# Layout of the normed x, order of the router products, and engine of the second tile's split in a one-core decoder step

## The reference, cut to what matters

```python
x = layernorm(x, ln_in_g, ln_in_b)
proj = x @ w_in                          # all q, k, v, gates of both head groups
h = concat(mlstm(proj...), hgrn2(proj...))     # two recurrent mixers, states returned
x = layernorm(ALPHA * x + h @ w_out, ln1_g, ln1_b)
logits = x @ w_router + b_router         # 32 experts, the best 4 taken, softmax over them
ffn = sum over chosen experts of gate * (((up + 1) * glu) @ w_down + b_down)
ple = sigmoid(x @ w_ple_gate) * (p @ w_ple_proj)
x = layernorm(ALPHA * x + ffn + ple, ln2_g, ln2_b)
```

## Time and profile before

| | |
|---|---|
| median of 3 runs | 1274.18 us (1273.34 to 1274.27) |
| the profiled execution | 1272.39 us |
| its span | 1270.6 us |
| PE busy | 1170.6 us (92%) |
| DVE, ACT, POOL busy | 356.0, 201.1, 84.8 us |
| moved by DMA | 442.84 MB, mean 349 GB/s |
| granted TensorE clock, mean | 0.973 |

### The profile page before, as it was taken

How to read it: one execution, slowest core, us unless ns; L and a number is a source line. 1 busy time by engine, 2 the same in 40 slices (tenths; PEclk the granted TensorE clock), 3 DMA queues, 4 the chain that set the end, 5 groups by cost and what they waited for, 6 DMA issues and landing times.

```text
span 1270.6 us, 13173 instructions
## 1 busy us (share of the span) xinstructions
PE 1170.6 (92%) x5601; PEld 488.8 (38%) x5601; DVE 356.0 (28%) x566; ACT 201.1 (16%) x322; POOL 84.8 (7%) x91
## 2 busy tenths in 40 slices
PE   4999999599999997899999999999999999998984
PEld 3677874544232322233323232323233232322221
DVE  6865324441212121111212121212122221203114
ACT  1344234641010101011000010101010000110000
POOL 4200130211000021000000000000000000000000
PEclk9999999699999998999999999999999999999997
DMA  9751121569999999999999999999999999999992
GB/s 299 232 154 67 67 90 44 198 269 359 423 420 422 421 421 387 407 421 422 419 415 419 421 420 421 406 421 421 422 420 420 421 421 411 421 420 421 373 421 84
DMA packets 71357, 442.84 MB, mean 349 GB/s; under 512 B 8320, under 2 KB 8992, under 8 KB 22144
## 3 DMA queue, kind: packets, MB, share of 16 engines
q1 hardware_dynamic: 65984, 425.92, 82.4%
q0 software_dynamic: 5312, 16.04, 3.8%
HBM read 437.19 MB, written 4.73 MB: 348 GB/s over the span
## 4 chain that ended last, share of the span: by engine, by line
PE 68%; DMA 18%; DVE 7%; ACT 4%; issue 1%; SPq 1%; POOL 1%; DVEq 0%
PE ps L1021 40%; DMA ring<-in_w_up 12%; PE ps L605 9%; PE ps L1002 5%; DMA ring<-in_w_gate 4%; PE ps L954 3%; DVE y_s L1857 2%; DMA ring<-in_w_down 2%; ACT xb L1169 2%; PE ps L633 2%; DVE h_s L1855 1%; PE ps L1009 1%; ACT hTe L1169 1%; PE ps L823 1%; PE ps L1037 1%
## 5 line engine op out<-in xcount | busy, mean ns | idle before, releaser
L1021 PE MATMUL ps<-ring,xTe 128*64 128x512 f32 x1536 | 358.6, 601 | 19.5 <-DMA ring<-in_w_up 14.1
L1021 PEld LDWEIGHTS ps<-ring,xTe 128*64 128x64 f32 x1536 | 105.5, 136 | 244.4 <-issue 244.2
L1021 PE MATMUL ps<-ring,hTe 128*64 128x512 f32 x768 | 178.9, 604 | 7.7 <-DMA ring<-in_w_down 7.7
L1837 DVE TENSOR_TENSOR xs<-xs,ps 128x512 f32<-128x512 f32 x64 | 43.9, 687 | 346.8 <-PE ps L1002 346.8
L1021 PE MATMUL ps<-more,xTe 128*64 128x512 f32 x496 | 113.5, 598 | 2.7 <-DMA more<-in_w_gate 2.1
L605 PE MATMUL ps<-xT,ring 128*128 128x288 f32 x448 | 115.0, 413 | 1.0 <-PE ps L605 0.6
L1021 PEld LDWEIGHTS ps<-ring,hTe 128*64 128x64 f32 x768 | 51.7, 138 | 121.2 <-issue 120.8
L605 PEld LDWEIGHTS ps<-xT,ring 128*128 128x128 f32 x448 | 84.7, 193 | 25.1 <-issue 2.3
L1002 PE MATMUL ps<-y_s,GT 128*128 128x512 f32 (+1 forms) x256 | 82.0, 519 | 2.2 <-ACT y_s L1169 1.2
L1855 DVE TENSOR_SCALAR h_s<-ps 128x512 f32<-128x512 f32 x32 | 21.8, 681 | 160.9 <-PE ps L1021 160.9
L1169 ACT ACTIVATE h_s<-g_s 128x1024 f32<-128x1024 f32 x16 | 16.9, 1056 | 310.9 <-DVE g_s L1845 310.9
(11 more groups left out here) (366 smaller groups left out, 856.5 us busy)
## 6 DMA issues: line engine op xcount, KB each, us to landing
ring<-in_w_gate SPq DMA_DIRECT2D x96, 1024.0 KB, 11.3
ring<-in_w_up SPq DMA_DIRECT2D x96, 1024.0 KB, 11.7
ring<-in_w_down SPq DMA_DIRECT2D x96, 1024.0 KB, 13.6
more<-in_w_gate SPq DMA_DIRECT2D x32, 1024.0 KB, 9.8
more<-in_w_down SPq DMA_DIRECT2D x32, 1024.0 KB, 13.0
more<-in_w_up SPq DMA_DIRECT2D x30, 1024.0 KB, 13.1
ring<-in_w_in SPq DMA_DIRECT2D x28, 512.0 KB, 6.0
ring<-in_w_out SPq DMA_DIRECT2D x8, 512.0 KB, 5.0
```

The lines of the kernel that those rows point to most:

```text
L1021: last = mm(ps[64 * q:64 * q + 64, bank0 + half, :], lhs(k, q), wide(t)[:, k % 2, half * 512:(half + 1) * 512], start=False, stop=k == KT - 1)
L1837: tt(x, x, ps[:, CB_BANKS[n], 0:512 if i < 2 else QW], ALU.add).then_inc(S["cb_added"], 1)
```

## The change

1. `x1` of tiles 0 and 1 is written in step order (k p) by the norm's last instruction, which reads x and the bias with a stride of 8 elements. ACT's parts, the subtractions and PE's transposes of it are then contiguous; the router weights for tiles 0 and 1 are loaded by (p kt). Tile 2 stays in natural order and gets a second copy of the router weights, `w_rq`, in the old layout. `copy_sample_rows` reads PSUM with a stride and writes runs of 64. The experts' residual start (`xs <- ALPHA * x1`) reads x1 with a stride.
2. PE's order: transposes of tile 0 half way through project_out(1), route(0) behind it, then transpose_keys_b and project_out(2). A third bank set for the keys.
3. Tile 1's subtractions move from POOL to DVE. ACT copies `xT` of tile 0 between its parts, and writes tile 1's later parts behind the square root of tile 2. DVE selects tile 0 before the residual of tile 2.
4. `ln_q` is copied from the full gains by eight ACT copies per norm; its 24 DMAs are gone. POOL's first wait is for the gains (`ln1_in`) and no longer for the sample rows.
5. `transpose_v` uses three banks for the first set.
6. The number of extra blocks is read before pair 1; DVE spreads tile 2's statistics before the branch, and PE sums them before it.

```diff
-                for q in range(4):
-                    sp.dma_start(ln_q[q * NS:(q + 1) * NS, n, :],
-                                 a[v][q * QW:(q + 1) * QW].partition_broadcast(NS)).then_inc(S["ln1_in"], 16)
...
-            pool.wait_ge(S["x_in2"], 64)
+            pool.wait_ge(S["ln1_in"], 32)
...
-                load_quarters("ln1_g", "ln1_b")
...
+            pool.wait_ge(S["sA_ok"], 1)
+                pool.dma_start(w_rq[:, :, :], a["w_router"][0].rearrange("(kt p) n -> p kt n", p=P)).then_inc(S["router_in"], 16)
...
-            for i in range(2):
-                for q in range(2):
-                    rest(i, q)
+            for q in range(2):
+                pool.wait_ge(S["part_ok"], q + 1)
+                out = rests[:, 0, :]
+                nc.gpsimd.tensor_tensor(out, out if q else x1[:, 0, :], xb[:, 0, q, :], ALU.subtract).then_inc(S["rest_ok"], 1)
...
-            load_quarters("ln2_g", "ln2_b")
...
-                    if base + i >= 2:
-                        pe.wait_ge(S["v_ok"], base + i - 1)
+                    if banks[i] in banks[0:i]:
+                        pe.wait_ge(S["v_ok"], base + banks.index(banks[i]) + 1)
...
             project_out(0)
             transpose_keys_a()
-            project_out(1)
+            project_out(1, lambda: transpose_normed(0))
+            route(0)
             transpose_keys_b()
-            transpose_normed(0)
             project_out(2)
+            pe.wait_ge(S["kbt_ok"], 3)
             transpose_normed(1)
             row_stats(2)
-            route(0)
             transpose_normed(2)
...
+                if p == 1:
+                    pe.wait_ge(S["pos_ok"], 1)
+                    extra = pe.value_load(n_exti[0:1, 0:1], min_val=0, max_val=NXP)
...
-            extra = pe.value_load(n_exti[0:1, 0:1], min_val=0, max_val=NXP)
+            row_stats(3)
...
+            def copy_quarters(g, b):
+                for n, v in enumerate((g, b)):
+                    for q in range(4):
+                        rows_q = slice(q * NS, (q + 1) * NS)
+                        last = f(ln_q[rows_q, n, :], v[rows_q, q * QW:(q + 1) * QW], ACT.Copy)
+                last.then_inc(S["ln_q_ok"], 1)
...
-                    f(by_row(xb[:, i, q, :]), natural(rests[:, i, :] if q else x1[:, i, :]), ACT.Copy).then_inc(S["part_ok"], 1)
+                    f(xb[:, i, q, :], rests[:, i, :] if q else x1[:, i, :], ACT.Copy).then_inc(S["part_ok"], 1)
...
-            for q in range(3):
-                part(0, q)
+            part(0, 0)
+            part(0, 1)
+            copy_xT(0, 6, 0)
+            part(0, 2)
...
-            copy_xT(0, 6, 0)
             norm_scale(1, 5)
             part(1, 0)
             copy_xT(1, 6, 0)
             norm_scale(2, 6)
+            part(1, 1)
             part(2, 0)
             copy_xT(2, 6, 0)
-            part(1, 1)
             part(2, 1)
+            part(1, 2)
             part(2, 2)
-            part(1, 2)
...
+                if 4 <= n < 6:
+                    last = stt(x1[:, i, :].rearrange("r (k p) -> r k p", k=KT), by_step(x), mv[:, i, 3:4], by_step(b),
+                               ALU.mult, ALU.add)
...
-            mixer_residual(2)
-            norm(2, 6)
...
             select(0)
-            rest_of_samples(0)
+            mixer_residual(2)
+            tile_stats(2)
+            spread_stats()
+            rest_of(1, 0)
+            norm_stats(2, 6)
+            norm_apply(2, 6)
+            rest_of(1, 1)
+            rest_of(2, 0)
             select(1)
-            rest_of_samples(1)
+            rest_of(2, 1)
             select(2)
...
+                if i < 2:
+                    step(ts(xs[:, i, :].rearrange("r (p k) -> r p k", k=KT), by_row(x1[:, i, :]), ALPHA, None, ALU.mult))
...
-            extra = dve.value_load(n_exti[0:1, 0:1], min_val=0, max_val=NXP)
+            spread_stats()
```

More of the change, by code:

```diff
@@ L215, in trunk_step @@
         ident_b, ident_s = sb("ident_b", [P, P], BF16), sb("ident_s", [3 * NS, NS], BF16)
+        w_rq = over("w_rq", [P, KT, NE], "masks", 0, "masks")
         ext = over("ext", [P, NEXTRA, NE], "rows", 4 * 4 * NT, "rows")
@@ L287, in by_row, with by_step @@
             return t.rearrange("r (k p) -> r p k", k=KT)
-        def natural(t):
-            return t.rearrange("r (p k) -> r p k", k=KT)
+        def by_step(t):
+            return t.rearrange("r (p k) -> r k p", k=KT)
         def tokens(i):
@@ L489, in _ @@
             pool.wait_ge(S["numB_mm"], 1)
+            pool.wait_ge(S["sA_ok"], 1)
+            with nc.allow_non_contiguous_dma(reason="router weights by rows of 128 bytes"):
+                pool.dma_start(w_rq[:, :, :], a["w_router"][0].rearrange("(kt p) n -> p kt n", p=P)).then_inc(S["router_in"], 16)
             nc.gpsimd.tensor_tensor(S0[:, :, :, :], S0[:, :, :, :],
@@ L1192, in _, with copy_values @@
                 norm_scale(i, i + 1)
+            act.wait_ge(S["ln1_in"], 32)
+            copy_quarters(ln_g, ln_b)
             for i in range(3):
                 copy_xT(i, 0, 6)
-            def copy_values(base, bank0, off, width):
+            def copy_values(base, banks, off, width):
                 for i, (_, r) in enumerate(TILES):
@@ L1225, in _ @@
                       scale=DKA ** -0.5 if buf is QK and j >= 2 else 1.0).then_inc(S["proj_ok"], 1)
+                if c == 3:
+                    act.wait_ge(S["ln2_in"], 32)
+                    act.wait_ge(S["x_norm"], 3)
+                    copy_quarters(ln_g, ln_b)
                 if c == 4:
@@ L1374, in _ @@
             for p in range(NPAIR):
+                if p == 1:
+                    act.wait_ge(S["pos_ok"], 1)
+                    extra = act.value_load(n_exti[0:1, 0:1], min_val=0, max_val=NXP)
                 if p >= 1:
@@ L1400, in _ @@
             copy_y(NPAIR - 1)
-            extra = act.value_load(n_exti[0:1, 0:1], min_val=0, max_val=NXP)
             with act.If(extra > 0):
@@ L1774, in _, with rest_of @@
             norm(1, 5)
-            mixer_residual(2)
-            norm(2, 6)
+            def rest_of(i, q):
+                if i == 1:
+                    dve.wait_ge(S["part_ok"], 3 + q + 1)
+                    tt(rests[:, 1, :], rests[:, 1, :] if q else x1[:, 1, :], xb[:, 1, q, :], ALU.subtract).then_inc(S["later_rest_ok"], 1)
+                else:
+                    dve.wait_ge(S["partq_ok"], q + 1)
+                    tt(rest_q[:, :], rest_q[:, :] if q else x1q[:, :], xbq[:, q, :], ALU.subtract).then_inc(S["later_rest_ok"], 1)
             def select(i):
@@ L1921, in _ @@
             for i, (_, r) in enumerate(TILES):
-                step(ts(tokens(i), normed(i), ALPHA, None, ALU.mult))
+                if i < 2:
+                    step(ts(xs[:, i, :].rearrange("r (p k) -> r p k", k=KT), by_row(x1[:, i, :]), ALPHA, None, ALU.mult))
+                else:
+                    step(ts(xq[:, :], x1q[:, :], ALPHA, None, ALU.mult))
             for p in range(NPAIR):
+                if p == 1:
+                    dve.wait_ge(S["pos_ok"], 1)
+                    extra = dve.value_load(n_exti[0:1, 0:1], min_val=0, max_val=NXP)
                 if p == 0:
```

71 lines of the change are left out of this document (32 added, 39 removed).

## The result

Median 1253.67 us (1252.57 to 1254.60, 4 runs) against 1273.76 us for the kernel before on the same chip: ratio 0.9843, 95% interval 0.9826 to 0.9860, a gain of 20.1 us. The forecast was 1257.2. The profiled execution took 1253.70 us; its span is 1251.8 us against 1270.6, so the two traces have 18.8 us to explain.

The account below looks back on a forecast made before the run. The weight stream, started by PE, paces the pairs; ahead of it stand startup waits, the values' bank wait, ACT's queue in stage 2 and the clock. 3.3 + 2.7 + 9.4 + 0.6 + 1.0 = 17.0 off 1274.18 gives 1257.2, range 1250 to 1264.

Parts of the forecast that it names:

- The likeliest case: Whole kernel: the forecast itself, 1257.2 us against the median, own range 1253 to 1261, given 67%.
- D: Expert pairs: weights late for their own reason, so the stream doesn't move; start, tail and routing gains gone, 1273; 4%.
- B: Start and values: masks or first weights late, or the values' wait returns as another; half of 6.0 lost, 1260; 14%.
- Start, 3.3: Program start: eight ln_q issues vanish around ln_b's load, first norm step at about 9.5 us; gain 3.3 (2.5 to 3.6).
- Values, 2.7: Values' transposes: a third bank removes the 2.69 us wait; gain 2.7 (bounds 0 and 2.7).
- Stage 2, 9.4: Project_out to first expert product: tiles 1 and 2 normed earlier, first expert product 265.93 to 256.5 on old scale; gain 9.4.
- 1.046 row: Profiled strided DVE instruction, 1.046 us for half the elements; used to size strided norm step and two residual starts at 2.09.
- rival A: Stage 2: the clock stays up, so routes, ranks, rows and states halve; about 8 us more, 1249; 8%.
- C: Stage 2 and pair 0: strides cost DVE what they cost ACT, 4.75 a norm step; 8 us back, 1265; 4%.
- E: Strided DVE instructions in stage 2 and pair 0: slower than before, deciding at 7.2 us each; 1277 at 8 us; 3%.
- Stream, 0.6: Weight stream: eight loads, 0.26 MB, leave the full DMA stretch; gain 0.6 us at 421 GB/s.
- End, 1.0: Kernel's end, DVE: only the branch remains before spreading statistics, beside PE's sum; gain 1.0 (bounds 0.3 and 1.5).

Follow-up runs that it names:

- work-at-the-start run: Changed kernel plus eight matmuls with unread results behind the first statistics product, where TensorE is idle from 8.9 to 13.6 us: 1251.86 us, ratio 0.9839.
- the two experiments: Kernel before with only three PSUM banks for the values' transposes, 1268.21 us; kernel before with that wait kept and three unread matmuls in it, 1270.95 us.
- The experiment: Changed kernel with route(0) moved from ahead of the second key transposes to behind the samples' projection: 1248.76 us, ratio 0.9812.
- the split back on GpSimd: Changed kernel with the second tile's two subtractions moved from DVE back to GpSimd, all else kept: 1252.94 us, ratio 0.9843.

## Why the prediction was right, and where it missed

*Direction and size.* 17.0 us forecast, 20.1 measured between medians and 18.8 between spans. The likeliest case came. That the sum came within 1.8 us of the spans is in part luck: its terms were off by 1.9, 3.4, 0.7, 0.9 and 0.5 us, and not all the same way. The pair stream moved with pair 0 (17.59 at its start, 17.28 at its end), against D; of B only the start came true.

*Start, 3.3: 1.35 measured.* Two steps failed. The load of ln_b took 6.26 us from issue to landing, so the first norm step began at 10.73 and not at 9.5. And 0.81 us more went in the first projections, which run at the slow rate until 24.2 to 24.6 us in both traces, whatever time they begin; I had read the projections as one block of 17.17 us and not seen that its first matmuls take 0.69 us and the later ones 0.41. The work-at-the-start run shows that this was there to be had. Eight quarter copies took 0.42 each (predicted 0.4), and the masks, late by 2.9 us on DVE, were covered as computed.

*Values, 2.7: 6.14 measured.* The wait was sized rightly (2.8 by the two experiments) and its follow-up was missed: the step "what is late next there is the product behind it" looked at operands and not at that product's own 3.42 us, where the one at 107 us had taken 2.02, nor at the 3.31 and 4.47 us of two groups further on. The clock fell to half at 117.0 us, 0.3 us behind the end of the wait, and once more at 127.3. This is the largest error of the sum, 3.4 us too little; the start, 1.9 too much, took more than half of it back.

*Stage 2, 9.4: 10.10 measured.* On the new scale (7.49 off) the steps foretold route(0) from 212.15, key transposes to 215.34, tile 1 at 220.76, the samples at 226.26 and the first product at 249.0; the trace has 211.83, about 215.0, 220.42, 225.7 and 248.34. The step taken from half the elements of another instruction, 2.09 us for the strided norm, took 2.05 and 2.08. That match owes something to luck: the instruction of the 1.046 row writes with a stride, the norm step reads with one, and the same row was well off for the residual's start. That the router products ahead of the key transposes put tile 1's norm on the path was in the working; that this cost outweighs what it brings was not drawn from it. The experiment draws it: 2.3 us at the mark, 1.2 of them in stage 2 ahead of the clock's return. The split on DVE was worth 0.3 us at most.

*Clock (rival A).* It fell and came back among the states as foretold; kept up by force to 230 us it gives 3 us, not the 8 I had given for it, since it then falls in the small products.

*Strides (C and E).* The strided DVE instructions cost 2.06 and 1.30 us, and the strided copies out of PSUM 0.59 us at 512 elements, no more than a contiguous copy of 512 (0.60). The Trainium skill, page "SBUF — State Buffer", section "Door 1: The DMA port swizzle", has an access that crosses to a new line of SBUF pay a penalty and a non-contiguous pattern in PSUM slow down matmuls. The rows agree for DVE's SBUF reads (2.06 against 1.29) and for ACT's bf16 parts (4.75 against 1.05). ACT's strided reads of PSUM show no penalty; no run here has a matmul to compare. The residual start costs 1.30 us each where I took 2.09; both were hidden, since the first and the second pair begin alike.

*Stream, 0.6: not seen.* The stretch of the pairs was 0.31 us longer, and in twelve traces it lies between 980.5 and 985.8. A term of that size had no place in the sum.

*End, 1.0: 1.51 measured*, at the upper bound: the 1.54 us of idle in front of the spread are gone, and the branch is hidden beside PE's sum as foretold.

## What to carry to other kernels

A wait of TensorE can have two prices: its own length, and a half clock that may follow; read the durations of the same instruction ahead of and behind the wait before sizing its removal. Where TensorE must wait anyway, put work there that stands later on the path: it fills the gap, leaves the path shorter and can keep the clock. And when one change has three parts, undo them one by one: here one carried the stage, one was worth next to nothing, and one cost 1.2 us or more. Where the clock falls and returns in the stretch that you compare, take the difference at a mark ahead of its return too: here the return alone moved a mark by 1 us.

## What the runs showed of the hardware

- Behind a wait of 2.69 us the granted clock fell to 0.50 (before, at 117.0 us, and again at 127.3); with 1.5 us of products in the wait it stayed at 1.00. In stage 2 of the changed kernel it fell at 222.3 us, in the second of three pieces of idle time (1.89, 1.59 and 1.93 us). It also fell with TensorE at work all along: among the router and rank products in four runs (at 230.0, 229.6, 226.4 and 225.9 us), and in one execution (the split back on GpSimd) among the projections at 136 us, where the changed kernel's clock stayed at 1.00 on the same code.
- At the start of the program TensorE works slowly with a recorded clock of 1.00: 0.69 us for a matmul that takes 0.41 from 24.5 us on; eight added products from 9 us on ended that before 19.3 us.
- A DVE instruction with two operands in SBUF that meets a tensor_tensor on GpSimd ended just behind it: a tensor_tensor of 0.18 us took 0.81, one of 0.42 took 1.97, a scalar_tensor_tensor of 0.49 took 1.83. One with a single SBUF operand kept its time (a tensor_reduce 0.37 us beside GpSimd's subtraction at 223.0).
- Strided fp32 reads cost DVE 2.06 instead of 1.29 us in a scalar_tensor_tensor of 1024 elements (both inputs strided) and 1.30 instead of 0.69 in a tensor_scalar; GpSimd's subtraction 2.85 instead of 2.13, DVE's 1.92 instead of 1.22.
